# Two blocks of a transformer on one core: scores that wait for the keys' bank alone, and differential outputs transposed into PSUM bank 6

## The reference, cut to what matters

```
A  diff attention, 4 heads:  logits of two maps of 64 columns each, causal, ALiBi
                             w = softmax(map 0) - lam * softmax(map 1);  y = w @ v
                             ya = rms_norm(y, diff_subln) * 0.2          (one head: 256 x 128)
C  forgetting attention, 4 heads of 128: logits + cum_q - cum_k, softmax, @ v
D  sliding window with sinks, 8 heads of 64 in 4 pairs, 2 key heads
gates = sigmoid(z_gate + b_gate)                 4 x 2048 columns
mixed = sum over n of gates[n] * (branch[n] @ w_branch[n]);  x = x + mixed @ w_out
```

## Time and profile before

| what | value |
|---|---|
| three timed runs | 4476.65, 4492.37, 4493.77 us |
| the profiled execution | 4476.64 us, its span 4474.9 us |
| PE busy | 4067.6 us (91%) |
| DVE, ACT, POOL busy | 2531.7 (57%), 2013.2 (45%), 222.1 us (5%) |
| mean granted TensorE clock | 0.945 |
| branches A, C, D of block one | from about 106 to 700 us of the span |

### The profile page before, as it was taken

How to read it: one execution, slowest core, us unless ns; L and a number is a source line. 1 busy time by engine, 2 the same in 40 slices (tenths; PEclk the granted TensorE clock), 3 DMA queues, 4 the chain that set the end, 5 groups by cost and what they waited for, 6 DMA issues and landing times.

```text
span 4474.9 us, 86039 instructions
## 1 busy us (share of the span) xinstructions
PE 4067.6 (91%) x34890; PEld 3999.7 (89%) x34890; DVE 2531.7 (57%) x3437; ACT 2013.2 (45%) x2753; POOL 222.1 (5%) x165
## 2 busy tenths in 40 slices
PE   7999999999999989999999789997399947999998
PEld 6889999999999989899999779997399947999998
DVE  5544555454444555446654555788945596554444
ACT  5444454455554444446544434453044413554443
POOL 0000000000000000000000000001700063000000
PEclk8999999999999999999999899998599957999999
DMA  4444445545555554433445334553045513555553
GB/s 161 160 151 160 161 170 180 178 160 196 189 195 179 196 164 151 160 132 132 142 152 187 105 113 169 195 190 140 0 169 196 189 47 104 192 192 179 187 187 122
DMA packets 106231, 708.67 MB, mean 158 GB/s; under 512 B 10864, under 2 KB 10992, under 8 KB 24144
## 3 DMA queue, kind: packets, MB, share of 16 engines
q1 hardware_dynamic: 105472, 701.55, 44.7%
q0 software_dynamic: 592, 4.72, 0.4%
HBM read 704.13 MB, written 2.10 MB: 158 GB/s over the span
## 4 chain that ended last, share of the span: by engine, by line
PE 87%; DVE 5%; issue 4%; ACT 3%; POOL 0%; DVEq 0%; POOLq 0%; ACTq 0%
PE ps L500 18%; PE ps L501 17%; PE ps L505 17%; PE ps L553 9%; PE ps L555 9%; PE ps L560 9%; PE ps L583 1%; DVE oh_r L2071 1%; PE ps L618 1%; ACT wh L1017 1%; PE ps L526 1%; PE ps L527 1%; PE ps L528 1%; DVE tmp L1526 1%; DVE oh_g L2078 1%
## 5 line engine op out<-in xcount | busy, mean ns | idle before, releaser
L1472 DVE TENSOR_TENSOR wl<-raw,wh 128x1024 fp32r<-128x1024 f32 x1328 | 1621.8, 1225 | 1645.5 <-ACT wh L1017 1629.8
L1017 ACT ACTIVATE wh<-raw 128x1024 fp32r<-128x1024 f32 x1328 | 1405.8, 1061 | 1927.2 <-PE ps L553 646.1
L500 PE MATMUL ps<-x,wh 128*128 128x256 f32 x6848 | 1646.6, 282 | 56.4 <-DVE x L1520 41.8
L501 PE MATMUL ps<-x,wh 128*128 128x256 f32 x6848 | 1631.4, 280 | 0.0
L500 PEld LDWEIGHTS ps<-x,wh 128*128 128x128 f32 x6848 | 1308.2, 191 | 68.4 <-issue 62.2
L501 PEld LDWEIGHTS ps<-x,wh 128*128 128x128 f32 x6848 | 1308.1, 191 | 0.6
L505 PE MATMUL ps<-x,wl 128*128 128x256 f32 x6848 | 929.2, 279 | 2.5 <-DVE wl L1472 2.5
L505 PEld LDWEIGHTS ps<-x,wl 128*128 128x128 f32 x6848 | 853.1, 190 | 2.8 <-DVE wl L1472 2.8
L553 PE MATMUL ps<-xkh,wh 128*128 128x256 f32 x3328 | 794.0, 280 | 23.9 <-DVE xkl L1483 23.9
L555 PE MATMUL ps<-xkl,wh 128*128 128x256 f32 x3328 | 793.1, 280 | 0.0
L553 PEld LDWEIGHTS ps<-xkh,wh 128*128 128x128 f32 x3328 | 634.1, 191 | 24.9 <-issue 24.9
(11 more groups left out here) (317 smaller groups left out, 2328.0 us busy)
## 6 DMA issues: line engine op xcount, KB each, us to landing
raw<-in_w_in SPq DMA_DIRECT2D x184, 1024.0 KB, 4.8
raw<-in_expert_u SPq DMA_DIRECT2D x128, 1024.0 KB, 4.8
raw<-in_expert_v SPq DMA_DIRECT2D x128, 1024.0 KB, 4.8
raw<-in_w_ffn_gate SPq DMA_DIRECT2D x44, 1024.0 KB, 4.8
raw<-in_w_ffn_up SPq DMA_DIRECT2D x44, 1024.0 KB, 4.8
raw<-in_w_ffn_down SPq DMA_DIRECT2D x44, 1024.0 KB, 4.8
raw<-in_w_out SPq DMA_DIRECT2D x32, 1024.0 KB, 4.8
raw<-in_w_branch SPq DMA_DIRECT2D x16, 1024.0 KB, 5.0
```

The source lines that it names most:

```text
L500: begin(mm(o, wh[:, j, c], xh[:, kc, :], start=kc == 0, stop=False), kc % 8 == 0)
L501: mm(o, wh[:, j, c], xl[:, kc, :], start=False, stop=False)
L1017: f(wh[:, u % 4, 0:width], raw[:, ring, c:c + width], ACT.Copy).then_inc(*k.up("hi"))
L1472: v.tensor_tensor(wl[:, u % 4, 0:width], raw[:, ring, c:c + width], wh[:, u % 4, 0:width].bitcast(F32), ALU.subtract).then_inc(*k.up("lo"))
```

## The change: what the waits are after it

```
@@ differential attention, per head
                 fill_gate(4 * h)
-                staged(0, 1)
+                staged(0)
                 for m in range(2):
                     qk(2 + m, qs[:, 0], ks[:, 0], 64 * m, 64 * m + 64)
...
                 pe.wait_ge(*k.next("a_y"))
-                reserve(7)
+                reserve(6)
                 for i in range(2):
-                    m = nc.tensor.transpose(ps[:, 7, i * P:(i + 1) * P], ysb[:, i, :], ident[:])
-                m.then_inc(*k.up("full_v7"))
+                    m = nc.tensor.transpose(ps[:, 6, i * P:(i + 1) * P], ysb[:, i, :], ident[:])
+                m.then_inc(*k.up("full_v6"))
@@ vector engine, differential heads, and once ahead of the forgetting heads
-                    take_y(7, Y_AT[0] + h - 1)
+                    take_y(6, Y_AT[0] + h - 1)
...
-                    take_y(7, Y_AT[0] + 3)
+                    take_y(6, Y_AT[0] + 3)
```

## The result

| | median of four runs | lowest to highest |
|---|---|---|
| before | 4488.47 us | 4476.65 to 4493.77 |
| changed | 4444.76 us | 4425.98 to 4457.35 |

Ratio 0.9899, with a 95% interval from 0.986 to 0.9939: the change takes 1.0% off, 0.6 to 1.4%. The predicted time was 4444 us.

The account below looks back on a forecast made before the run. PE was taken to bound the kernel (87% of the chain); 26.1 + 8.0 + 5.9 + 2.8 - 2 = 40.8 us saved gave 4436 us from the profiled run, 4452 from the median; predicted the middle, 4444, range 4422 to 4462.

Parts of the forecast that it names:

- idle before the scores: PE's waits at L618, twelve places in the three branches, vanish wholly: 26.1 us saved.
- output transposes: At L681, four places, PE starts 1.47 us earlier once only a_y is awaited: 5.9 us saved.
- The clock term: Lower clock after five 3.0 us score stalls and two L681 waits goes: 8.0 and 2.8 us saved.
- The remaining wait at L681: Before the output transposes about 0.95 us of stall stays, ended by DVE's L1660.
- the allowance for the pace: PE's two matmul paces near the change, 3.9% apart: 2 us loss taken, bounds 7 us lost to 11 won.
- rival 3: A long stage, such as the expert table's at 3300 us, goes slow: 14 to 28 us lost; chance 0.08.
- the saving outside 100 to 700 us is over 10 us either way: Sign that the prediction is wrong; the other was a saving inside that is not 35 to 50 us.
- Rival 1: Score stall moves to a later wait at L630; about 18 us saved, 4458 to 4474; chance 0.05.
- Rival 5: Nothing gained at L618's five "issue" waits, their cause unnamed; 27 us saved, 4449 to 4466; chance 0.05.
- Rivals 2 and 4: 2: last stage goes fast, 55 us saved, chance 0.10. 4: everything fast goes slow, 57 us slower, 0.02.

Follow-up runs that it names:

- e3: Changed kernel again, nothing edited, for another profile; 4437.3 us, ratio 0.9899.
- e9: Changed kernel with output transposes one tile later on PE and groups of three short PE operations in u0, v0, u1, v1; 4431.89 us, ratio 0.9899.
- e8: Kernel before again, nothing edited, for one more profile; 4476.69 us in one run.
- e11: Changed kernel again, nothing edited, for a third profile; 4432.83 us in one run.
- e2: Kernel before with only the output transposes and their reader moved to bank 6; 4481.72 us, ratio 0.998.
- e1: Kernel before with only the three staged(0, 1) made staged(0); 4450.45 us, ratio 0.9919.
- e5: Changed kernel with ACT repeating the first gate tile's sigmoid seven times in each differential head before releasing bank 1; 4431.97 us, ratio 0.9898.

## Why the prediction was right

**Time and mechanism.** 4444 us was forecast and 4444.76 measured; such closeness is luck, since single runs of one kernel, taken together, lie 43 us (e3) to 56 us (before, beside e9) apart. What can be checked more sharply is the part up to L553:

| term | forecast | measured, first pair of profiles |
|---|---|---|
| idle before the scores, twelve places | 26.1 | 27.3, from start to start |
| output transposes, four places | 5.9 | 6.2 |
| clock, seven places, and pace near by | 8.0 + 2.8 - 2 | 12.3, the rest of 45.8 |
| sum | 40.8 | 45.8 (42.9 for e8, 810.3, against e3 and e11, their mean 767.5) |

The idle time was right to the edge that a stall adds: a matmul's modelled end is later than the next one can start. The remaining wait at L681 was put at 0.95 us and is 0.87.

**The clock term.** It was a little too small: seven low stretches at 1.4 to 1.6 us each made 10.8 us, where the granted clock of 0.95 over 240 us gives 12. The price of each was met (8.23 against 6.62 or 6.83 us in A). With the 1.4 us by which the allowance for the pace was too large (below), that is most of the 3.5 us between 8.8 and 12.3. What the prediction didn't see is that the same wait doesn't always cost the same: each of the fifteen waits of 3.0 us in before, e8 and e2 went with the lower clock, three of them for twice as long, and of the twelve waits of 2.43 us in before, e8 and e1 seven did. None of 1.6 us or less did. So in these profiles each half of the change came out worth less alone than in the sum. The granted clock in after is 1.00 from 120 to 360 us, so the loss behind waits for a copy out of PSUM was real. The Trainium skill ("TensorE: Matmul & The Clock Gate", section "Loop structure matters more than you think") says that such a copy doesn't break PE's warmth, in a loop where the next matmuls follow immediately; carried over to this kernel the sum would have been about 32 us. The runs show that it doesn't carry over to a PE that sits idle for the copy.

**The pace was the right unknown, at the wrong place.** Near the change it cost next to nothing: in before the slow distances between 90 us and L553 add up to about 14.5 us over the fast pace, in after to about 15.1, so 0.6 us where I took 2. Far from it, it decides what a single run shows. The prediction gave 0.08 to a long stage going slow (rival 3); that happened in the profile taken, 27 us, and its own test "the saving outside 100 to 700 us is over 10 us either way" came out against it. The error was to treat the pace as something a change may shift once and for all. e3 and e11 show u0 and v0 fast in the same program that had them slow, and e8 shows ffn and v1 changed in the kernel before. So one profile can't tell what an edit does to a long stage; only v1, slow three times of three, leaves that open.

**The rivals.** Rival 1 (the stall moves) is refuted by after and by e5: the chain hangs on PE, with a margin that was estimated at 1.0 us on ACT and is 1.3. Rival 5 (unnamed waits stay) is refuted: the five "issue" waits went with the others. Rivals 2 and 4 didn't occur.

## What to carry to other kernels

A wait list that is longer than what the instruction reads is the first thing to look for when PE idles at the same instruction again and again: compare what ended the wait with what the operands need. Follow the chain behind the freed wait to the point where it is tied to the engine that got faster; if it is tied there, the saving stays. Measure a small saving at a mark just behind the edit as well as in the total, and don't take the clock's share of two edits, measured one by one, as their sum.

## What the runs showed of the hardware

Matmuls of 256 fp32r columns at the full clock follow each other at 113.3 ns or at 117.8 ns, for hundreds of microseconds at a time, with the same instructions (851 or 885 in 100 us). A long stage can have either in different runs of one program, at 13 to 19 us a stage in the table above. Groups of three 128-column fp32 matmuls or transposes turned slow into fast in most cases and fast into slow almost never; what the state is stays open.

Not all of it is drawn. The products of `fill_mix` (L526 to L528), in which one matmul with `wl` follows each pair with `wh`, ran at the slow pace in all thirteen profiles, some 1304 distances in each and at most one at the fast pace. Where such a product follows one of `tile_T`, which uses `wl` eight times in a row at its end, the pace can change without a stall, another width or a change of clock. From before, whose granted clock is 1.00 from 2150 to 2155 us:

```profile
2152.13 0.62 PE L505 MATMUL ps<-x,wl 128*128 128x256 f32 x4
2152.58 0.28 PE L526 MATMUL ps<-y,wh 128*128 128x256 f32 x1
...
2153.29 0.28 PE L526 MATMUL ps<-y,wh 128*128 128x256 f32 x1
```

The four of L505 take 0.45 us from start to start, 113 ns each; the next six take 0.71 us, 118 ns each. No run changed the order of these products, so whether the order is the cause stays open; at 4.5 us for every thousand matmuls it is worth a try.

The lower clock came with every wait of 3.0 us, with seven of twelve of 2.43 us and with none of 0.7 to 1.6 us, in the profiles of before, e8, e1, e2, the changed kernel and e5.
